# A reordered chunk plan, banks for the token range, later rotations, and the compressed layers' weights behind the gates' first slot

## The chip, the cores and the metric

The kernel runs on one core of a Trainium2 chip. The metric is the device time of one execution in microseconds (us), the median of three runs. The five engines of the core are told of by their names in the profile: PE is TensorE's matmul (PEld its weight load), DVE is VectorE, ACT is ScalarE, POOL is GpSimd, and SP is SyncE, which here only issues transfers.

## The reference

Two transformer blocks on a batch of one, 256 tokens of width 1024, all in float32. The first mixes a three-group attention and an RWKV-like recurrence, with a feed-forward layer and a gated embedding behind them. The second, on which most of the change lies, begins so:

```python
p = _split_columns(u @ w_in)          # q_a k_a v_a q_b k_b ... q_c k_cmp v_cmp k_sel v_sel ... g_merge
o_a = _stick_breaking(q_a, k_a, v_a)
o_b = _dsa_attention(_rope(q_b), rope1(k_b), v_b, _rope(q_idx), rope1(k_idx), w_idx)
o_c = _nsa_attention(_rope(q_c), rope1(k_cmp), v_cmp, rope1(k_sel), v_sel, rope1(k_win), v_win, gates_c, cmp...)
g = sigmoid(g_merge)                  # 3 x 1024 columns
merged = g[0] * (o_a @ w_up[0]) + g[1] * (o_b @ w_up[1]) + g[2] * (o_c @ w_up[2])
```

and inside `_nsa_attention` keys and values are compressed: 15 overlapping blocks of 32 tokens by 64 features go through `gelu(blocks @ w1) @ w2`, with w1 of 2048 by 128 (1 MB) once for keys and once for values.

## The kernel before, in words

**Products in parts.** A float32 product is made of three matmuls on rounded parts: each operand is split into a high part (written by ScalarE, line 1808, type fp32r) and a low part (VectorE subtracts the high part from the whole, line 2705), and TensorE takes high x high, high x low and low x high (lines 716 to 718, or 794, 795 and 803). So before TensorE can use a weight slot, three things happen in a row: its transfer lands, ScalarE copies it, VectorE subtracts. Both do so in halves of the contraction, `(j, 0)` and `(j, 1)`. The high parts have two buffers, so the split of slot j waits for the last matmul of slot j - 2.

**Streams and slots.** The weights of a stage are a stream of slots of up to 1 MB, held in a ring of three places; SP loads them in order (`load`, line 610), each one waiting until TensorE has finished the slot that held the place before. For the second block's input projection (`st2`) the slots are: 0 to 4, the feature chunks n = 2 to 6 of `plan_2` (features on the partitions, 256 tokens in the free dimension); 5 and 6, the token range (tokens on the partitions, 464 columns: values, gates' inputs, index weights); 7 to 18, six gate column ranges of two slots each. Chunks n = 0 and 1 were made in `head`, before.

**Feature chunks.** A chunk of 256 columns has two halves of 128, one of 128 columns has one. Behind a chunk, ScalarE reads the bank (one plain copy and four that swap 32-row groups, `rope_read`), and VectorE rotates it one chunk later with cosines, sines and an add (`rope`, lines 2806, 2808 and 2810). Chunk n = 4 is the third group's query, n = 5 the four single keys (k_b, k_idx, k_sel, k_win in 64-column pieces), n = 6 the compressed layers' input (128 columns). Chunks and token range take banks 0 and 1 in turn.

**The early split.** `ahead` (scalar program): for slot 5 of `st2`, ScalarE makes the first half's high part before it reads the chunk of n = 5, not after.

**Key copies.** `scores` needs the single keys in both halves of the partitions. ScalarE copies three times behind the chunk n = 6, VectorE three times when it reads the token range (`read_vt`).

**Turns.** The gates are then computed by `turns.drive(gates_main(), nsa_keys(), dsa(1), dsa(0), stick())`. Every engine runs the same schedule: one step of the main work (on TensorE six matmuls of a gate slot, four steps to a slot), then one step of a side work, the four sides in turn. So turn 1 is a step of slot 7 and a step of `nsa_keys`, turn 2 a step and `dsa(1)`, turn 3 with `dsa(0)`, turn 4 with `stick`, and turn 5 begins slot 8 with `nsa_keys` again. All engines execute in order. In turns 1 and 2, ScalarE's main step is the split of slot 8 in two halves; after the second, in turn 2, it applies the ReLU to the scores of `dsa(1)`. The sides share the banks 2, 3 and 4 in rotation: `dsa(1)` takes 2 and 3, `dsa(0)` 4 and 2.

**The compressed layers.** `nsa_keys`: POOL adds the position vector for 15 blocks (line 3837) once the rotation of the compressed input is there. In its second step (turn 5), TensorE takes 64 small products of the blocks with w1 (line 1597) into banks 5 and 6, in four row groups of 32; in its fourth step (turn 13) it turns and sums these groups with eight products against pieces of the identity (line 1607), then two last products. The transfers of w1 (four of 512 KB, in rows of 512 bytes) and of w2 (four of 32 KB) are issued on SP behind slot 1 (`if j == 1`, line 669), in practice at the start of the stage. The gate ranges from the third on write where w1 lay and wait for its products.

**The first block's part.** While TensorE works on the q/k chunks of the first block (`qkv`, six chunks), the RWKV recurrence runs beside them as side work in an order written out by hand (`order_1`); its masked copies on VectorE are lines 2993 and 2969. VectorE rotates chunk n - 1 at the end of chunk n (`rope1`), in two buffers `rt1`.

**Activation tables.** ScalarE loads a table set before a function that the current set does not hold; the stick-breaking side uses Abs, Exp and Ln in turn 12.

Of the kernel before, what the change touches and what calls it, by code (L numbers as in the profile page):

```python
# [33 lines left out]
C_END = C_SINC + 256  # L34
# [10 lines left out]
def shape_constants():  # L45
# [37 lines left out]
    c[0:64, C_SINC:C_SINC + 256] = np.concatenate([-sin, sin])  # L83
    return c
# [189 lines left out]
def program(nc, A, consts, vecs, pt, out):  # L274
    with ExitStack() as ctx:
# [75 lines left out]
        sm_nsa = [(small(4), small(4), small(4), small(4)) for _ in range(2)]  # L351
        sm_mem = [(small(4), small(4), small(4)) for _ in range(2)]
# [36 lines left out]
        rt1 = [view3(P + 9216 + 1024 * i, 2, 256) for i in range(2)]  # L389
# [36 lines left out]
        def rope_to(n):  # L426


            return RC[:, 6:10:3, :] if n == 5 else RC[:, 10:11, :] if n == 6 else RC[:, 2 * (n - 2):2 * (n - 2) + 2, :]
# [45 lines left out]
        def rslot3(n, nk, width):  # L475
# [8 lines left out]
                  ([(1152, 256, 0)], [128, 128]), ([(1476, 256, 0)], [128, 128]),  # L484
                  ([(1024, 64, 0), (1408, 64, 64), (1860, 64, 128), (1988, 64, 192)], [128, 128]), ([(1732, 128, 0)], [128])]
# [111 lines left out]
        def sync_program(e):  # L597
# [105 lines left out]
        def tensor_program(e, turns):  # L703
# [131 lines left out]
            def token_range(st, j0, n, w, freed, late):  # L835
                nk = 8 // n
                banks = [next(pg), next(pg)]
# [700 lines left out]
            def scores(done, name, i, qc, kc_, W, freed):  # L1538
# [3 lines left out]
                q.wait_ge(*rope_dve.at("in2", 5))  # L1542
# [44 lines left out]
            def nsa_keys():  # L1587
                yield
# [30 lines left out]
            def nsa(i):  # L1619
# [7 lines left out]
                q.wait_ge(*rope_dve.at("in2", 4))  # L1627
# [167 lines left out]
        def scalar_program(e, turns):  # L1795
# [78 lines left out]
            def ahead(st, j):  # L1874

                return st.tag == "st2" and j == 5
# [13 lines left out]
            def token_range(st, j0, n, read):  # L1890
                nk = 8 // n
                banks = [next(pg), next(pg)]
                for s in range(n):
                    for i in range(2):
                        for r in range(nk // 2):
                            if i == 0 and (r == 1 or r == 0 and not ahead(st, j0 + s + 1)):
# [85 lines left out]
            def rope_read(tag, n, m, b, zs, dst):  # L1982
                if n >= (2 if tag == "qk" else 4):
                    q.wait_ge(*rope_dve.at(tag, n - 2))
# [4 lines left out]
            def qkv():  # L1989
# [9 lines left out]
                for n in range(6):  # L1999
                    b = next(pg)  # L2000
                    yield from feature_chunk(st1, QK_AT + n, [128, 128], lambda: rope_read("qk", n, 2, b, rt1[n % 2], qk[:, 2 * n:2 * n + 2, :]))
# [358 lines left out]
            def read2(n, b):  # L2360
                if n < 2:
                    copy(QA[:, 2 * n:2 * n + 2, :], halves(bank(b))).then_inc(main_act.up("qa", n), 1)
                else:
                    m = 1 if n == 6 else 2
# [4 lines left out]
            def read_vt(i, p):  # L2369
                copy(vt[:, i, 0:256], p[:, 0:256])  # L2370
                act(g12[:, 12 * i:12 * i + 12], p[:, 448:460], ACT.Tanh, scale=0.5).then_inc(main_act.up("vt2", i), 1)

            def main_b():
                for n in range(2, 7):
                    b = next(pg)
                    yield from feature_chunk(st2, n - 2, plan_2[n][1], lambda: read2(n, b))
                    if n == 6:
                        q.wait_ge(*rope_dve.at("in2", 5))
                        for m, half in enumerate(half_rows[::-1]):
                            copy(RC[half, 7, :], RC[half_rows[1], 6, :]).then_inc(key_act.up(m), 1)  # L2380
                        q.wait_ge(*key_act.at(1))
                        copy(RC[half_rows[1], 6, :], RC[half_rows[0], 6, :]).then_inc(key_act.up(2), 1)
                yield from token_range(st2, 5, 2, read_vt)

            turns.alone(main_b())


# [228 lines left out]
        def vector_program(e, turns):  # L2616
# [127 lines left out]
            def token_range(st, j0, n, read, late):  # L2744
                nk = 8 // n
                banks = [next(pg), next(pg)]
# [64 lines left out]

            def rope1(n):
                rope("qk", n, 2, rt1[n % 2], qk[:, 2 * n:2 * n + 2, :], C_COS, C_SIN)

            def qkv():
# [474 lines left out]
            def rope2(n):  # L3290
                if n >= 2:
                    m = 1 if n == 6 else 2
                    rope("in2", n, m, rz2[n % 2][:, 0:m, :], rope_to(n), *((C_COSC, C_SINC) if n == 6 else (C_COS, C_SIN)))

            def read_vt(i, p):
                if i == 0:
                    q.wait_ge(*rope_dve.at("in2", 5))
# [9 lines left out]
            def main_b():  # L3307
# [3 lines left out]
                yield from token_range(st2, 5, 2, read_vt, lambda: rope2(6))  # L3311
# [341 lines left out]
        def gpsimd_program(e, turns):  # L3653
# [177 lines left out]
            def nsa_keys():  # L3831
# [3 lines left out]
                q.wait_ge(*rope_dve.at("in2", 6))  # L3835
# [126 lines left out]
```

## Time and profile before

| | |
|---|---|
| median of 3 runs | 909.4 us (909.09 to 910.02) |
| the profiled execution | 909.91 us |
| its span | 907.4 us |
| TensorE busy | 882.2 us, 97% |
| VectorE busy | 606.8 us, 67% |
| ScalarE busy | 480.5 us, 53% |
| transfers | 150.71 MB, mean 166 GB/s |

The span is what the profile shows of the execution; the time has 2.5 us more around it. In the timeline, a row is: start, duration, engine, line, operation, output and input, shape, count, and in brackets how long the engine had been idle and what ended it. Rows of one kind next to each other are merged, and the duration is then that of all. A window's row is: from and to, its length, the busy time (and instructions) of PE, PEld, DVE, ACT and POOL, PE's granted clock as a share of 2.4 GHz, the DMA share and the GB/s.

### The profile page before, as it was taken

What the parts mean: (1) busy time and instruction counts of PE and PEld (TensorE: products, weight loads), DVE (VectorE), ACT (ScalarE), POOL (GpSimd) and SP (SyncE); (2) the same over time, 40 slices, a digit from 0 to 9 for tenths busy, and PEclk for the clock granted to TensorE, in tenths of its full rate; (3) what the DMA queues carried; (4) which work ended last, traced back from release to release, by engine and by line L of the source; (5) the groups of instructions that cost most, each with busy time, mean ns of one, the idle gap of its engine ahead of it and who ended that gap; (6) DMA issues with size and microseconds to landing.
All of it is one profiled execution on the core that took longest, in us unless ns stands there. A gap on an engine that the chain in (4) does not pass through costs nothing.

```text
span 907.4 us, 15435 instructions
## 1 busy us (share of the span) xinstructions
PE 882.2 (97%) x6552; PEld 748.8 (83%) x6552; DVE 606.8 (67%) x976; ACT 480.5 (53%) x775; POOL 29.2 (3%) x51
## 2 busy tenths in 40 slices
PE   7999999999899999999999999999999999999997
PEld 4999898787689888888889978776788788888885
DVE  4578978557856666656766577877863566666673
ACT  4775667436534444456444856484622545555561
POOL 0010000010000000000000020000000000000000
PEclk9999999999999999999999999999999999999999
DMA  9644333224468665555339764353817566665521
GB/s 336 190 140 140 99 119 114 63 83 150 178 248 282 188 190 190 200 202 187 121 112 229 164 210 144 111 186 107 277 38 206 146 187 188 191 193 194 199 95 47
DMA packets 131204, 150.71 MB, mean 166 GB/s; under 512 B 11808, under 2 KB 102176, under 8 KB 131008
## 3 DMA queue, kind: packets, MB, share of 16 engines
q1 hardware_dynamic: 129920, 145.57, 51.8%
q10 hardware_dynamic: 1216, 4.16, 1.2%
q8 instruction: 52, 0.85, 0.4%
q14 instruction: 16, 0.13, 0.0%
HBM read 148.67 MB, written 1.05 MB: 165 GB/s over the span
## 4 chain that ended last, share of the span: by engine, by line
PE 85%; DVE 7%; ACT 4%; issue 2%; DMA 1%; POOL 0%; POOLq 0%; ACTq 0%; DVEq 0%
PE psum L821 12%; PE psum L716 9%; PE psum L718 9%; PE psum L717 9%; PE psum L826 7%; PE psum L774 4%; PE psum L794 3%; PE psum L795 3%; PE psum L803 3%; PE psum L722 3%; PE psum L870 2%; PE psum L880 2%; PE psum L871 2%; PE psum L827 2%; DVE parts L2705 2%
## 5 line engine op out<-in xcount | busy, mean ns | idle before, releaser
L1808 ACT ACTIVATE parts<-low 128x1024 fp32r<-128x1024 f32 (+3 forms) x252 | 254.3, 1044 | 65.6 <-PE psum L718 48.3
L2705 DVE TENSOR_TENSOR parts<-low,parts 128x1024 fp32r<-128x1024 f32 (+3 forms) x156 | 183.7, 1206 | 37.7 <-ACT parts L1808 37.5
L716 PE MATMUL psum<-parts 128*128 128x512 f32 (+2 forms) x424 | 169.1, 399 | 4.6 <-DVE parts L2705 2.5
L718 PE MATMUL psum<-parts 128*128 128x512 f32 (+2 forms) x424 | 163.5, 386 | 0.0
L717 PE MATMUL psum<-parts 128*128 128x512 f32 (+2 forms) x424 | 163.4, 385 | 0.0
L1808 ACT ACTIVATE high<-psum 128x512 f32<-128x512 f32 (+6 forms) x115 | 63.4, 560 | 134.2 <-PE psum L827 76.4
L821 PE MATMUL psum<-parts 128*128 128x512 f32 x462 | 116.8, 392 | 0.0
L716 PEld LDWEIGHTS psum<-parts 128*128 128x128 f32 x424 | 79.6, 188 | 26.3 <-DVE parts L2705 4.5
L821 PEld LDWEIGHTS psum<-parts 128*128 128x128 f32 x462 | 86.9, 188 | 16.9
L718 PEld LDWEIGHTS psum<-parts 128*128 128x128 f32 x424 | 79.6, 188 | 16.4
L717 PEld LDWEIGHTS psum<-parts 128*128 128x128 f32 x424 | 79.8, 188 | 13.9
L2770 DVE TENSOR_TENSOR parts<-low,parts 128x1024 fp32r<-128x1024 f32 x54 | 66.0, 1222 | 35.3 <-ACT parts L1808 35.3
L794 PE MATMUL psum<-parts 128*128 128x256 f32 (+2 forms) x312 | 79.0, 291 | 0.0
L795 PE MATMUL psum<-parts 128*128 128x256 f32 (+2 forms) x312 | 76.5, 282 | 0.0
L826 PEld LDWEIGHTS psum<-parts 128*128 128x128 f32 x528 | 72.0, 190 | 5.1
L826 PE MATMUL psum<-parts 128*128 128x256 f32 x528 | 73.6, 282 | 0.0
L794 PEld LDWEIGHTS psum<-parts 128*128 128x128 f32 (+2 forms) x312 | 58.9, 189 | 2.2 <-issue 1.2
L795 PEld LDWEIGHTS psum<-parts 128*128 128x128 f32 (+2 forms) x312 | 59.0, 189 | 0.3 <-issue 0.3
L3197 DVE TENSOR_TENSOR mid<-psum,high 128x512 f32<-128x512 f32 x33 | 22.8, 692 | 46.2 <-ACT high L1808 46.2
L1808 ACT ACTIVATE mid<-psum 32x512 f32<-32x512 f32 (+7 forms) x61 | 32.9, 552 | 31.5 <-PE psum L803 12.9
L803 PE MATMUL psum<-parts 128*128 128x256 f32 (+2 forms) x312 | 43.8, 283 | 0.0
L803 PEld LDWEIGHTS psum<-parts 128*128 128x128 f32 (+2 forms) x312 | 40.1, 189 | 0.0
(313 smaller groups left out, 1310.6 us busy)
## 6 DMA issues: line engine op xcount, KB each, us to landing
low<-in_w_in_dram SPq DMA_DIRECT2D x40, 1024.0 KB, 5.3
low<-in_w_ffn_in_dram SPq DMA_DIRECT2D x44, 512.0 KB, 5.2
low<-in_w_ff_in_dram SPq DMA_DIRECT2D x16, 1024.0 KB, 5.7
low<-in_w_ff_out_dram SPq DMA_DIRECT2D x16, 1024.0 KB, 4.8
low<-in_w_ffn_out_dram SPq DMA_DIRECT2D x11, 1024.0 KB, 5.0
low<-in_w_out_dram SPq DMA_DIRECT2D x8, 1024.0 KB, 5.2
low<-in_w_ple_gate_dram SPq DMA_DIRECT2D x4, 1024.0 KB, 5.0
low<-consts_dram ACTq DMA_DIRECT2D x1, 2078.0 KB, 9.0
```

What stands on the lines that cost most here:

```text
L716: mm(o, l[0], r[0], start, False)
L717: mm(o, l[0], r[1], False, False)
L718: return mm(o, l[1], r[0], False, stop)
L774: t = mm(PSUM[0:m, banks[n], 256 * j + 128 * i:256 * j + 128 * i + 128], w3[:, k, off:off + m], uT[:, k, 128 * i:128 * i + 128], k == 0, k ...
L794: mm(o, hi[:, k, c], st.uh[:, k, :], k == 0, False)
L795: mm(o, lo_[:, k, c], st.uh[:, k, :], False, False)
L803: t = mm(o, hi[:, k, c], st.ul[:, k, :], False, k == 7)
L821: mm(p, hi[:, k, c], st.u2(k), k == 0, False)
L826: mm(p[:, 0:256], lo_[:, k, c], st.uh[:, k, :], False, False)
L1808: return e.activation(o, a, ACT.Copy)
L2705: tt(rslot3(n, nk, width)[:, r, 0:w], slot3(n, nk, width)[:, r, 0:w], st.hi3(j)[:, r, 0:w].bitcast(F32), ALU.subtract) \
L2770: tt(rview(OR + 2048 * n + 1024 * (k % 2), 1024), slot(n)[:, 1024 * (k % 2):1024 * (k % 2) + 1024], rview(base, 1024).bitcast(F32), ALU.su ...
```

## The change

- In `plan_2` the order of the last three chunks becomes: single keys (n = 4, slot 2), compressed input (n = 5, slot 3, 128 columns), third group's query (n = 6, slot 4). What depends on the numbers (`rope_to`, the waits of `scores` and `nsa`, POOL's wait, `read_vt`) follows.
- The token range of `st2` uses banks 5 and 6.
- `ahead` is gone: every split comes in the plain order.
- ScalarE's three key copies move from behind the last chunk into `read_vt`, row block 0.
- The first step of `nsa_keys` on TensorE no longer yields, so its 64 products come in turn 1 instead of turn 5; a yield is added behind them, so the later steps keep their turns.
- The summing of the four row groups takes one product per half against a selection matrix `C_SEL` (128 more columns of constants, 64 KB) instead of four.
- The transfers of w1 and w2 are issued behind slot 7 instead of slot 1.
- In the first block, `rt1` has four buffers, and `turned_at` sets which rotations stand at the end of chunk n: none, none, 0, 1, 2 and 3, 4 (and 5 in the gates, as before).
- One Exp of one column (`first_exp`) on ScalarE ahead of the turns.

```diff
-C_END = C_SINC + 256
+C_SEL = C_SINC + 256
+C_END = C_SEL + 128
...
+    c[:, C_SEL:C_SEL + 16] = r % 32 == s[:, 0:16]
...
-        rt1 = [view3(P + 9216 + 1024 * i, 2, 256) for i in range(2)]
+        rt1 = [view3(P + 8704 + 512 * i, 2, 256) for i in range(4)]
...
         plan_2 = [([(0, 256, 0)], [128, 128]), ([(256, 256, 0)], [128, 128]), ([(768, 256, 0)], [128, 128]),
-                  ([(1152, 256, 0)], [128, 128]), ([(1476, 256, 0)], [128, 128]),
-                  ([(1024, 64, 0), (1408, 64, 64), (1860, 64, 128), (1988, 64, 192)], [128, 128]), ([(1732, 128, 0)], [128])]
+                  ([(1152, 256, 0)], [128, 128]), ([(1024, 64, 0), (1408, 64, 64), (1860, 64, 128), (1988, 64, 192)], [128, 128]),
+                  ([(1732, 128, 0)], [128]), ([(1476, 256, 0)], [128, 128])]
...
                 load(("st2", j), (3, 0, 5)[j % 3], [cols(*p) for p in pieces], main_pe.at("st2", j, 1))
-                if j == 1:
+                if j == 7:
                     q.wait_ge(*wo_pe.at("pg", "y", 1, 1))
...
-                yield from token_range(st2, 5, 2, 464, lambda i: [main_act.at("vt2", i), main_dve.at("vt2", i)], nothing)
+                yield from token_range(st2, 5, 2, 464, lambda i: [main_act.at("vt2", i), main_dve.at("vt2", i)], nothing, (5, 6))
...
             def nsa_keys():
-                yield
                 p = [bank(5), bank(6)]
...
                 yield
                 yield
+                yield
                 p = bank(7)
                 for h in range(2):
                     q.wait_ge(*cmp_dve.at("x", h))
-                    for g in range(4):
-                        t = mm(p[:, 16 * h:16 * h + 16], hd[:, h, :], ident[:, 32 * g:32 * g + 16], g == 0, g == 3)
+                    t = mm(p[:, 16 * h:16 * h + 16], hd[:, h, :], const(C_SEL, 16), True, True)
...
                 for n in range(steps):
-                    if n == 1 or n == 0 and not ahead(st, j + 1):
+                    if n < 2:
                         split(st, j + 1, (n,))
                     yield
                 q.wait_ge(*main_pe.at(st.tag, j, 1))
-                if ahead(st, j + 2):
-                    split(st, j + 2, (0,))
                 read()
...
             def read_vt(i, p):
+                if i == 0:
+                    q.wait_ge(*rope_dve.at("in2", 4))
+                    for m, half in enumerate(half_rows[::-1]):
+                        copy(RC[half, 7, :], RC[half_rows[1], 6, :]).then_inc(key_act.up(m), 1)
+                    q.wait_ge(*key_act.at(1))
+                    copy(RC[half_rows[1], 6, :], RC[half_rows[0], 6, :]).then_inc(key_act.up(2), 1)
...
             turns.alone(main_b())
+            act(first_exp, ident[:, 0:1], ACT.Exp).then_inc(stick_act.up("table"), 1)
...
+            turned_at = ((), (), (0,), (1,), (2, 3), (4,))
...
-                    yield from feature_chunk(st1, QK_AT + n, [128, 128], (lambda n=n: rope1(n - 1)) if n else nothing, nothing)
+                    yield from feature_chunk(st1, QK_AT + n, [128, 128], lambda n=n: [rope1(m) for m in turned_at[n]], nothing)
```

## Rows read from the trace of the kernel before

**Rows 1.** The page, busy time of the engines, share of the span, instructions

```profile
PE 882.2 (97%) x6552; PEld 748.8 (83%) x6552; DVE 606.8 (67%) x976; ACT 480.5 (53%) x775; POOL 29.2 (3%) x51
```

**Rows 2.** Timeline of TensorE and VectorE in the first block's q/k chunks

```profile
103.72 1.12 PE L803 MATMUL psum<-parts 128*128 128x256 f32 x8
105.87 0.24 PE L1203 MATMUL psum<-high 64*64 64x64 f32 x1 [1.04 <-DVE high L2993]
107.19 0.24 PE L1203 MATMUL psum<-mid,high 64*64 64x64 f32 x1 [0.16 <-DVE high L2969]
...
100.95 0.69 DVE L2806 TENSOR_TENSOR mid<-mid,low 128x512 f32<-128x512 f32 x1
102.88 2.84 DVE L2993 TENSOR_TENSOR high<-psum,low 64x512 f32<-64x512 f32 x4
...
133.82 2.85 DVE L2993 TENSOR_TENSOR high<-psum,low 64x512 f32<-64x512 f32 x4 [2.62 <-PE psum L1181]
```

**Rows 3.** Timeline of the second block's chunks and token range

```profile
502.20 2.01 ACT L1808 ACTIVATE parts<-low 128x1024 fp32r<-128x1024 f32 x2
503.29 2.36 DVE L2705 TENSOR_TENSOR parts<-low,parts 128x1024 fp32r<-128x1024 f32 x2 [5.96 <-ACT parts L1808]
510.81 3.02 ACT L1808 ACTIVATE high<-psum 128x512 f32<-128x512 f32 x5 [0.84 <-PE psum L803]
515.42 1.12 PE L803 MATMUL psum<-parts 128*128 128x256 f32 x8
518.30 1.12 PE L803 MATMUL psum<-parts 128*128 128x256 f32 x8
520.66 0.48 PE L716 MATMUL psum<-parts 128*128 128x464 f32 x1 [1.24 <-ACT high L1808]
522.82 0.48 PE L716 MATMUL psum<-parts 128*128 128x464 f32 x1 [0.63 <-DVE parts L2705]
528.37 0.48 PE L716 MATMUL psum<-parts 128*128 128x464 f32 x1 [1.49 <-DVE parts L2705]
```

**Rows 4.** SP's issue, two issues with us to landing, two windows

```profile
486.56 2.47 SPq L669 DMA_DIRECT2D high<-in_cmp_w_v_dram  x1
high<-in_cmp_w_v_dram SPq DMA_DIRECT2D x1, 512.0 KB, 11.5
low<-in_w_in_dram SPq DMA_DIRECT2D x1, 1024.0 KB, 4.9
488.00:494.00 6.00, 6.00 (x55) 6.00 (x55) 4.10 (x4) 3.13 (x6) 0.00 (x0) 1.00 1.21 203
529.00:531.00 2.00, 2.00 (x11) 1.78 (x10) 1.97 (x4) 0.80 (x1) 2.00 (x4) 1.00 1.04 406
```

**Rows 5.** Timeline of the turns and the blocks; two lines' ns min/median/max, starts

```profile
536.37 1.13 PE L1548 MATMUL psum<-high 64*128 64x256 f32 x8
539.01 0.38 PE L1548 MATMUL psum<-high 64*128 64x128 f32 x2
537.53 1.09 ACT L1804 ACTIVATE mid<-psum 128x512 f32<-128x512 f32 x2 [1.44 <-PE psum L1548]
525.90 6.09 POOL L3837 TENSOR_TENSOR mid<-high,low 128x32 f32<-128x32 f32 x15 [41.46 <-DVE high L2810]
L1597 PE MATMUL psum<-high,mid x128: 269/269/293, 544.7 to 546.4; 64*32 64x128 f32 x128
L1607 PE MATMUL psum<-low,mid x16: 177/263/263, 557.6 to 559.2; 128*128 128x16 f32 x16
```

**Rows 6.** Timeline of table load and last matmul; two windows (clock third last)

```profile
554.94 1.28 ACT L1804 ACT_TABLE_LOAD   x1
901.01 0.39 PE L718 MATMUL psum<-parts 128*128 128x512 f32 x1
...
560.56:583.60 23.04, 22.21 (x118) 17.28 (x117) 21.12 (x63) 10.97 (x18) 0.00 (x0) 1.00 0.32 100
904.00:905.00 1.00, 0.00 (x0) 0.00 (x0) 0.30 (x1) 0.46 (x1) 0.00 (x0) 0.56 0.00 0
```

More of the change, by code:

```diff
@@ L351, in program @@
         sm_nsa = [(small(4), small(4), small(4), small(4)) for _ in range(2)]
+        first_exp = small(1)
         sm_mem = [(small(4), small(4), small(4)) for _ in range(2)]
@@ L426, in rope_to @@
         def rope_to(n):
-            return RC[:, 6:10:3, :] if n == 5 else RC[:, 10:11, :] if n == 6 else RC[:, 2 * (n - 2):2 * (n - 2) + 2, :]
+            return RC[:, 6:10:3, :] if n == 4 else RC[:, 10:11, :] if n == 5 else RC[:, 4:6, :] if n == 6 else RC[:, 2 * (n - 2):2 * (n - 2) + 2, :]
         vt = view3(P + 21760, 2, 660)
@@ L833, in wide_chunk, with token_range @@
                 yield
-            def token_range(st, j0, n, w, freed, late):
+            def token_range(st, j0, n, w, freed, late, banks=None):
                 nk = 8 // n
-                banks = [next(pg), next(pg)]
+                banks = banks or [next(pg), next(pg)]
                 for s in range(n):
@@ L1541, in scores @@
                     bank(b)
-                q.wait_ge(*rope_dve.at("in2", 5))
+                q.wait_ge(*rope_dve.at("in2", 6))
                 q.wait_ge(*key_act.at(2))
@@ L1626, in nsa @@
                     bank(b)
-                q.wait_ge(*rope_dve.at("in2", 4))
+                q.wait_ge(*rope_dve.at("in2", 6))
                 q.wait_ge(*cmp_act.at("kc"))
@@ L1872, in head @@
                             read(n)
-            def ahead(st, j):
-                return st.tag == "st2" and j == 5
             def feature_chunk(st, j, widths, read):
@@ L1884, in feature_chunk, with token_range @@
                 q.wait_ge(*main_pe.at(st.tag, j, 1))
-                if ahead(st, j + 2):
-                    split(st, j + 2, (0,))
                 read()
                 yield
-            def token_range(st, j0, n, read):
+            def token_range(st, j0, n, read, banks=None):
                 nk = 8 // n
-                banks = [next(pg), next(pg)]
+                banks = banks or [next(pg), next(pg)]
                 for s in range(n):
@@ L1895, in token_range @@
                         for r in range(nk // 2):
-                            if i == 0 and (r == 1 or r == 0 and not ahead(st, j0 + s + 1)):
+                            if i == 0 and r < 2:
                                 split(st, j0 + s + 1, (r,))
@@ L1982, in rope_read @@
             def rope_read(tag, n, m, b, zs, dst):
-                if n >= (2 if tag == "qk" else 4):
-                    q.wait_ge(*rope_dve.at(tag, n - 2))
+                if n >= 4:
+                    q.wait_ge(*rope_dve.at(tag, n - (4 if tag == "qk" else 2)))
                 z = halves(bank(b))[:, 0:m, :]
@@ L2000, in qkv @@
                     b = next(pg)
-                    yield from feature_chunk(st1, QK_AT + n, [128, 128], lambda: rope_read("qk", n, 2, b, rt1[n % 2], qk[:, 2 * n:2 * n + 2, :]))
+                    yield from feature_chunk(st1, QK_AT + n, [128, 128], lambda: rope_read("qk", n, 2, b, rt1[n % 4], qk[:, 2 * n:2 * n + 2, :]))
             def gate(r):
@@ L2363, in read2 @@
                 else:
-                    m = 1 if n == 6 else 2
+                    m = 1 if n == 5 else 2
                     rope_read("in2", n, m, b, rz2[n % 2][:, 0:m, :], rope_to(n))
@@ L2376, in main_b @@
                     yield from feature_chunk(st2, n - 2, plan_2[n][1], lambda: read2(n, b))
[L2377 to L2383, printed above, removed]
+                yield from token_range(st2, 5, 2, read_vt, (5, 6))
             turns.alone(main_b())
+            act(first_exp, ident[:, 0:1], ACT.Exp).then_inc(stick_act.up("table"), 1)
             pa2 = itertools.cycle((2, 3, 4))
@@ L2742, in feature_chunk, with token_range @@
                 yield
-            def token_range(st, j0, n, read, late):
+            def token_range(st, j0, n, read, late, banks=None):
                 nk = 8 // n
-                banks = [next(pg), next(pg)]
+                banks = banks or [next(pg), next(pg)]
                 for s in range(n):
@@ L3291, in rope2 @@
                 if n >= 2:
-                    m = 1 if n == 6 else 2
-                    rope("in2", n, m, rz2[n % 2][:, 0:m, :], rope_to(n), *((C_COSC, C_SINC) if n == 6 else (C_COS, C_SIN)))
+                    m = 1 if n == 5 else 2
+                    rope("in2", n, m, rz2[n % 2][:, 0:m, :], rope_to(n), *((C_COSC, C_SINC) if n == 5 else (C_COS, C_SIN)))
             def read_vt(i, p):
                 if i == 0:
-                    q.wait_ge(*rope_dve.at("in2", 5))
+                    q.wait_ge(*rope_dve.at("in2", 4))
                     for m, half in enumerate(half_rows):
@@ L3310, in main_b @@
                     yield from feature_chunk(st2, n - 2, plan_2[n][1], lambda: rope2(n - 1), nothing)
-                yield from token_range(st2, 5, 2, read_vt, lambda: rope2(6))
+                yield from token_range(st2, 5, 2, read_vt, lambda: rope2(6), (5, 6))
             turns.alone(main_b())
@@ L3834, in nsa_keys @@
                 e.memset(blk[:, :, 15:32], 0.0).then_inc(cmp_pool.up("pad"), 1)
-                q.wait_ge(*rope_dve.at("in2", 6))
+                q.wait_ge(*rope_dve.at("in2", 5))
                 for n in range(15):
```

2 lines of the change are left out of this document (1 added, 1 removed).

## The prediction

> **What bounds the kernel now.** Read first the page's busy times, then the rows in which TensorE had nothing to do. TensorE is busy 97% of the span [rows 1], so a microsecond of its work or of its idleness is nearly a microsecond of the kernel; the other engines matter only where TensorE waits for them. The change touches two stretches where it does. A wait in the rows counts from the modelled end of the matmul before, which overlaps the next one by about 0.2 us; I therefore price waits from start to start.
>
> In the first block's q/k chunks, TensorE stops at 105.87 and 107.19 for VectorE [rows 2]. Eight products at L803 take 1.05 us to the next start (0.13 each), so without the waits the products at 105.87 would begin at 104.8. VectorE was late because it ran the rotation of q/k chunk 0 (100.95 to 102.9, three operations of 0.69) before the masked copies at 102.88.
>
> In the second block's chunks, a half chunk (128 columns of weight) takes TensorE 2.88 us, from 515.42 to 518.30 [rows 3], a whole one 5.76. The last ends at 519.3. The token range after it begins at 520.66, 1.4 late (its bank is still being read by ScalarE); it stops again at 522.82, 0.8, and at 528.37, 1.65, for VectorE's low parts [rows 3]. Together 3.8 us.
>
> **The change, step by step.** Times are those of the profile of before, so that the shifts can be added.
>
> *Rotations in the first block.* Rotation 0 goes one chunk later, and the masked copies start when the low parts are done, at about 100.95 instead of 102.88: 1.9 us earlier. Both TensorE waits (1.1 + 0.2) go: **-1.3**. Chunk 4 gets two rotations, 2.0 us more on VectorE; the cover is the 2.62 us in which VectorE idles before 133.82 [rows 2]. Without it, up to 2 us would return.
>
> *Banks 5 and 6 for the token range, the key copies moved into it, the early split given up.* The bank wait goes, and since the query chunk is now last, the other two waits change form. The old 3.8 us are taken out, **-3.8**, and the new ones counted:
>
> The half chunk is now the last but one. ScalarE reads chunk n=4 from 510.81 for 3.02 us and only then splits the weights of n=6, 1.0 us per half, VectorE taking 1.2 for each low part [rows 3]: first low part at 510.81 + 3.02 + 1.0 + 1.2 = 516.1. TensorE finishes the half chunk at 513.4: **+2.7**, and +0.1 for the second part. The query chunk ends at 516.1 + 0.1 + 5.8 = 522.0. ScalarE reads it until 525.1; VectorE finishes its rotation (two more operations of 0.65) and then the low part of slot 6 (1.1) at 527.6. TensorE has done slot 5 (24 matmuls at 0.21) at 527.1: **+0.6**. Slot 6 ends at 532.9, and the first turn's six matmuls at 534.4.
>
> *The compressed layers' weights.* They leave SP's queue ahead of the chunks' weights (no TensorE wait there hangs on a load) and enter it behind slot 7. Slot 7's load waits for the query chunk's last matmul, so it goes out at 522.1. Between issue and landing of a lone 1 MB load lie 4.9 us, 2.6 of them data at 406 GB/s, so 2.3 us are not [rows 4]. The four 512 KB transfers run in rows of 512 bytes at 203 GB/s [rows 4]: 2.1 MB take 10.4 us. The four small ones I put at 0.8, between 0.3 at 406 and 1.3 at half of 203 (their rows are 256 bytes). Then the up-projection's 1 MB and slot 8's 1 MB, 2.6 each. One queue serves them in order, so the compressed weights land near 522.1 + 2.3 + 2.6 + 10.4 = 537.4, and slot 8 at 537.4 + 0.8 + 5.2 = 543.4. What SP is held up by its full queue is inside this: the last quarter's issue began at 486.56, and it landed 11.5 us after [rows 4], so SP runs ahead of the data.
>
> *Who waits.* TensorE reaches the compressed products at 534.4 and stands about 3.1 us. POOL's blocks, 6.1 us [rows 5] from about 522.7, are done; the reads of banks 5 and 6 end about a microsecond after slot 6. But behind slot 8 hangs more: ScalarE, in order, splits slot 8 in turns 1 and 2 before the ReLU that frees the bank which `dsa(0)` wants in turn 3. Landing 543.4, two splits 2.0, one ReLU 0.55 (half of 1.09 [rows 5]): the bank is free at 546.1. Unhindered, TensorE would be there earlier: the `dsa(1)` scores and six matmuls take 2.64 (536.37 to 539.01), 1.1 of it the scores, the compressed products 2.0 (544.7 to 546.4 and the last one's 0.27) [rows 5]; 534.4 + 2.0 + 1.6 + 2.6 = 540.7, with 0.1 for the changes of kind. So the two stops together are **+5.4**, whatever part of them the first takes. Slot 8's low parts are ready before its matmuls at 550.1, and the loads of 9 and 10 follow in time (546 for a need near 550).
>
> *Small products.* Moving them to turn 1 costs nothing by itself. The hidden rows' turning falls from eight products (16 passes, 557.6 to 559.3 [rows 5]) to two: 1.7 x 6/8 = **-1.3**. From 560.56, where ScalarE's Ln lets it go, VectorE is busy 21.1 of 23.0 us [rows 6]; this saving is kept only if that chain also moves. The early Exp does that: it shifts one table load (1.28 us at 554.94 [rows 6]) to before turn 1, where ScalarE waits for slot 8 anyway. Bounds: kept 1.3, or nothing. I take it kept. The constants' 64 KB more are 0.2 us of queue under other loads, the rest has one answer: nothing.
>
> Sum: -1.3 - 3.8 + 2.8 + 0.6 + 5.4 - 1.3 = **+2.4 us**. The profiled execution took 909.9 us, 907.4 of it span, half a microsecond above the median of 909.4; on the median the forecast is 911.8.
>
> **Rivals.** *The transfers run faster than 203 GB/s.* The 203 were measured for these very rows, and the queue was full; against it speaks only that wider rows reach 406 [rows 4]. At that pace they take 5.2, not 10.4, slot 8 lands at 538.2, the bank is free at 540.9, and 0.2 us are left of the 5.4: 909.4 - 2.8 = 906.6, faster. It decides once slot 8 has landed by 538, where its ReLU no longer ends behind TensorE's arrival at 540.7. The Trainium skill, in "DMA: Bandwidth & Descriptors", section Bandwidth, measured 341 GB/s for a 1 MB transfer; by that figure, an estimate, the four would take 6.2 us and the kernel 907.7. No run here shows that pace for rows of 512 bytes.
>
> *TensorE's clock falls in the stop.* At the end of the kernel the last matmul starts at 901.01; at 904 to 905 the granted clock is 0.56, on its way from 2.4 to 1.2 GHz [rows 6]. A stop of 3.1 us is about as long. At half clock the 6.3 us of work up to the second stop would take 12.6, of which the second stop (2.3) swallows that much: at most +4.0, 915.8. If the low clock lasts through 2.3 us of work or less, it costs nothing. "TensorE: Matmul & The Clock Gate", section on the HAM clock gate, in the Trainium skill says that an idle stretch halves the clock until TensorE has been busy again for a while; the trace's fall to 0.56 agrees, and no row here shows a fall between two stages.
>
> *VectorE's full stretch eats the small gains.* If the table load stays where it is, or the compressed products' earlier place leaves VectorE behind, the 1.3 are lost and up to 1 us more: 913.1 to 914.1. For it speaks that VectorE is so full there [rows 6]; against it that ScalarE's 1.28 match TensorE's 1.3.
>
> *The stops are smaller than counted*, because the queue takes the transfers partly side by side, half of the 5.4: 909.1, no change.
>
> **How the numbers follow.** A measurement can tell 0.2%, 1.8 us: faster is below 907.6, slower above 911.2. My forecast has 0.60 (its own range 910.8 to 913.4, from landing times of slot 8 off by 1 us and the early Exp at half its worth; 0.05 of it falls within 0.2%), the fast transfers 0.11 (0.09 faster, 0.02 same), the clock 0.09, VectorE 0.11, the smaller stops 0.09. That makes faster 0.09, same 0.16, slower 0.75. For the range I leave out most of the fast case and the clock's upper end: 908.9 to 914.8.
>
> **What would show it.** Right: no wait at the old 105.87; a TensorE wait of 2.5 us for VectorE before the query chunk; none for ScalarE at the token range's start; a wait of about 3 us ahead of L1597's products, released by the DMA of the compressed weights; a second of about 2.3 us at a score product, released by ScalarE's ReLU, with ScalarE idle about 9 us for slot 8's load; no table load between Abs and Exp. Wrong: slot 8's landing less than 17 us after the query chunk, or a clock below 1.00 after the first stop.

## The result, and the profile after

The changed kernel takes **915.4 us** (median of 4 runs, 913.8 to 915.99) against 909.5 of the kernel before on the same chip: a ratio of 1.0064, 95% interval 1.0052 to 1.0076. It is slower, as forecast, but by 5.9 us where the forecast had 2.4, and the time lies 0.6 above the range. The profiled execution took 915.99 us, its span 914.0, so it stands 6.6 above the span of before; the ledger below explains those 6.6.

The page of the changed kernel, which answers to [rows 1]:

```profile
PE 884.0 (97%) x6540; PEld 749.9 (82%) x6540; DVE 606.7 (66%) x976; ACT 480.6 (53%) x776; POOL 26.6 (3%) x51
```

TensorE is busy 1.8 us longer with twelve matmuls fewer. Some matmuls must have become slower; the other 4.8 us are idle time. The timeline of TensorE, the answer to [rows 3]:

```profile
516.27 0.36 PE L797 MATMUL psum<-parts 128*128 128x256 f32 x1 [2.67 <-ACT high L1810]
516.46 0.28 PE L798 MATMUL psum<-parts 128*128 128x256 f32 x1
...
517.71 0.41 PE L797 MATMUL psum<-parts 128*128 128x256 f32 x1
517.92 0.41 PE L798 MATMUL psum<-parts 128*128 128x256 f32 x1
...
519.41 1.47 PE L806 MATMUL psum<-parts 128*128 128x256 f32 x8
...
523.59 0.37 PE L719 MATMUL psum<-parts 128*128 128x464 f32 x1
...
529.35 0.48 PE L719 MATMUL psum<-parts 128*128 128x464 f32 x1 [0.55 <-DVE parts L2702]
```

The token range's start no longer waits, and the query chunk waits instead. Its first matmuls follow each other at 0.12 us, those from 516.85 to 519.4 at 0.21. The windows show why (clock third from the end):

```profile
513.00:516.00 3.00, 0.60 (x6) 0.40 (x4) 1.10 (x1) 2.94 (x5) 0.00 (x0) 1.00 1.16 284
516.00:517.00 1.00, 0.73 (x5) 0.76 (x6) 1.00 (x2) 0.96 (x3) 0.00 (x0) 0.88 1.04 348
517.00:518.00 1.00, 1.00 (x7) 1.00 (x6) 1.00 (x3) 0.95 (x4) 0.00 (x0) 0.50 1.20 293
...
519.00:520.00 1.00, 1.00 (x6) 1.00 (x6) 1.00 (x2) 0.65 (x1) 0.00 (x0) 0.50 0.07 9
520.00:521.00 1.00, 1.00 (x10) 1.00 (x9) 1.00 (x2) 0.00 (x0) 0.00 (x0) 0.91 0.00 0
```

From about 516.8 to 520.2, starting half a microsecond after TensorE has resumed from its stop, the granted clock is 0.50, 1.2 instead of 2.4 GHz. The chunk takes 7.32 us (516.27 to 523.59) instead of the 5.76 of before.

The turns, TensorE, ScalarE and SP's issue, the answer to [rows 4, 5]:

```profile
539.68 2.90 PE L1599 MATMUL psum<-high,mid 64*32 64x128 f32 x128 [3.64 <-DMA high<-in_cmp_w_v_dram]
542.51 0.80 PE L719 MATMUL psum<-parts 128*128 128x512 f32 x1
...
549.00 0.71 PE L1551 MATMUL psum<-high 64*128 64x128 f32 x8 [1.46 <-ACT mid L1806]
...
535.18 1.28 ACT L1806 ACT_TABLE_LOAD   x1
536.47 0.20 ACT L1806 ACTIVATE low<-low 128x1 f32<-128x1 f32 x1
546.46 2.00 ACT L1810 ACTIVATE parts<-low 128x1024 fp32r<-128x1024 f32 x2 [9.79 <-DMA low<-in_w_in_dram]
548.37 1.06 ACT L1806 ACTIVATE mid<-psum 128x512 f32<-128x512 f32 x2
...
523.79 0.37 SPq L613 DMA_DIRECT2D low<-in_w_in_dram  x1
524.20 1.44 SPq L672 DMA_DIRECT2D high<-in_cmp_w_k_dram  x2
525.68 6.07 SPq L672 DMA_DIRECT2D high<-in_cmp_w_v_dram  x2
```

Both stops are where they were forecast and for the reasons forecast. Slot 8 reaches ScalarE at 546.46, not 543.4. The clock is at 0.50 once more, from 540.7 to 544.1: the small products take 2.83 us from start to start (539.68 to 542.51) instead of 1.96 in the kernel before. That fall costs nothing, because the second stop ends when ScalarE is ready, however fast TensorE gets there.

### The profile page after: what moved, and what is told of

Its sections match the earlier page's. It is cut to its first block, busy times and chain, and to the rows that moved or that the text cites. A ratio compares the mean times of both kernels' runs of the same rounds, so it can differ in the third digit from the quotient of the medians.

```text
span 914.0 us, 15410 instructions
## 1 busy us (share of the span) xinstructions
PE 884.0 (97%) x6540; PEld 749.9 (82%) x6540; DVE 606.7 (66%) x976; ACT 480.6 (53%) x776; POOL 26.6 (3%) x51
## 3 DMA queue, kind: packets, MB, share of 16 engines
HBM read 148.73 MB, written 1.05 MB: 164 GB/s over the span
## 4 chain that ended last, share of the span: by engine, by line
PE 84%; DVE 7%; ACT 3%; DMA 2%; issue 2%; SPq 1%; POOL 0%; POOLq 0%; ACTq 0%; DVEq 0%
PE psum L824 12%; PE psum L719 9%; PE psum L721 8%; PE psum L720 8%; PE psum L829 7%; PE psum L797 4%; PE psum L777 4%; PE psum L798 3%; PE psum L806 3%; PE psum L725 3%; PE psum L873 2%; PE psum L883 2%; PE psum L874 2%; DVE parts L2702 2%; PE psum L830 2%
## 5 line engine op out<-in xcount | busy, mean ns | idle before, releaser
L1810 ACT ACTIVATE parts<-low 128x1024 fp32r<-128x1024 f32 (+2 forms) x252 | 254.2, 1044 | 74.9 <-PE psum L721 48.2
L2702 DVE TENSOR_TENSOR parts<-low,parts 128x1024 fp32r<-128x1024 f32 (+2 forms) x156 | 183.5, 1206 | 44.6 <-ACT parts L1810 44.3
L797 PE MATMUL psum<-parts 128*128 128x256 f32 (+2 forms) x312 | 80.1, 293 | 2.7 <-ACT high L1810 2.7
L798 PE MATMUL psum<-parts 128*128 128x256 f32 (+2 forms) x312 | 77.6, 285 | 0.0
L797 PEld LDWEIGHTS psum<-parts 128*128 128x128 f32 (+2 forms) x312 | 59.6, 191 | 5.0 <-ACT high L1810 2.8
L798 PEld LDWEIGHTS psum<-parts 128*128 128x128 f32 (+2 forms) x312 | 59.8, 192 | 0.3 <-issue 0.3
L806 PE MATMUL psum<-parts 128*128 128x256 f32 (+2 forms) x312 | 44.1, 284 | 0.0
L806 PEld LDWEIGHTS psum<-parts 128*128 128x128 f32 (+2 forms) x312 | 40.5, 191 | 0.0
```

The costliest lines, as they stand in the source:

```text
L797: mm(o, hi[:, k, c], st.uh[:, k, :], k == 0, False)
L798: mm(o, lo_[:, k, c], st.uh[:, k, :], False, False)
L806: t = mm(o, hi[:, k, c], st.ul[:, k, :], False, k == 7)
L1810: return e.activation(o, a, ACT.Copy)
L2702: tt(rslot3(n, nk, width)[:, r, 0:w], slot3(n, nk, width)[:, r, 0:w], st.hi3(j)[:, r, 0:w].bitcast(F32), ALU.subtract) \
```

## The experiments

Experiments 1 to 3 ask what the late transfers cost and how, 4 asks for the first block's part, 5 to 7 for the stop before the query chunk, 8 and 9 for the small products, and 10 and 11 for slot 8's landing. "Before" is always the kernel before, on the same chip. A distance from the changed kernel's 915.4 or between two experiments can be one between chips; on all of them the kernel before took 909.2 to 909.5.

**1. Transfers back behind slot 1, all else as changed.**

```diff
-                if j == 7:
+                if j == 1:
```

> The changed kernel with one line put back: the compressed layers' transfers are issued behind slot 1 again. Theory T (the transfers behind slot 7 cost both stops in the turns): the wait of 3.64 us for the compressed weights and the one of 1.46 us for ScalarE's ReLU go, 6.9 us from start to start, so 915.4 - 6.9 = 908.5 us; the stop of 2.7 us before the query chunk stays, and with it the fall of TensorE's clock, which now nothing downstream hides. Rival C (the new chunk order and the clock make the loss, the transfers are hidden anyway): 913 us or more.

Measured: 910.2 us, ratio to before 1.0010 (1.0002 to 1.0019). The late transfers cost 5.2 us net, and both stops in the turns are gone. What the expectation (908.5) missed is a stop elsewhere, shown by TensorE's timeline, and behind it the old one; ScalarE's row shows what the first waited for:

```profile
506.19 0.36 PE L797 MATMUL psum<-parts 128*128 128x256 f32 x1 [1.62 <-DVE parts L2702]
...
517.83 0.36 PE L797 MATMUL psum<-parts 128*128 128x256 f32 x1 [2.65 <-ACT high L1810]
...
536.77 2.02 PE L1599 MATMUL psum<-high,mid 64*32 64x128 f32 x128 [0.48 <-DVE low L2623]
...
503.73 2.00 ACT L1810 ACTIVATE parts<-low 128x1024 fp32r<-128x1024 f32 x2 [1.87 <-DMA low<-in_w_in_dram]
```

Slot 2 was as large before and stood behind the same 2.1 MB, and nobody waited for it. But then it was one piece of 256 columns, and the transfers ran at 303 and 349 GB/s from 497 to 499; now it is the keys' four pieces of 64 columns, in rows of 256 bytes, and the same two microseconds show 181 and 134. That the row size sets this pace is argued, no run varies it alone. Experiment 6 takes up the place in the queue.

**2. The kernel before, transfers behind slot 7.** The same line, `j == 1` made `j == 7`; the small products stay in turn 5.

> The kernel before with only the transfers moved behind slot 7; the compressed products stay in turn 5. Theory T (the price is set by slot 8's landing, through ScalarE's ReLU in turn 3, not by the wait for the compressed weights): no TensorE wait for the weights in turn 5, but one of 6 to 7.5 us in turn 3; 909.5 + 6 to 7.5 = 915.5 to 917 us. Rival W (the loss is the wait of the first turn for the weights themselves): with the products in turn 5 the weights are there, and the time stays within 1 us of 909.5.

Measured: 919.8 us, 10.5 above before, ratio 1.0112 (1.0099 to 1.0126). No product waits for its weights; the price is the wait behind slot 8 and ScalarE, as theory T has it, and 3 us that the expectation (915.5 to 917) lacked:

```profile
546.26 1.23 PE L1548 MATMUL psum<-high 64*128 64x128 f32 x8 [6.74 <-ACT mid L1804]
547.42 0.79 PE L716 MATMUL psum<-parts 128*128 128x512 f32 x1
```

Its windows around and behind that stop:

```profile
543.00:546.00 3.00, 0.00 (x0) 0.00 (x0) 1.19 (x1) 2.28 (x3) 0.00 (x0) 0.50 0.86 315
546.00:552.00 6.00, 5.74 (x23) 4.48 (x25) 4.42 (x10) 2.91 (x6) 0.00 (x0) 0.50 0.11 18
553.00:556.00 3.00, 3.00 (x94) 2.34 (x99) 2.98 (x5) 0.00 (x0) 0.00 (x0) 1.00 0.57 221
```

Of the 10.2 us of span, 6.7 are the stop and 3 are lost in some 6 us of work at half clock behind it (546.3 to 552.6). The other 0.5 was lost far from the edit, where the clock also fell, behind a stop that the kernel before has too (1.75 us there, without a fall):

```profile
230.73 0.51 PE L1395 MATMUL psum<-parts 128*128 128x512 f32 x1 [1.84 <-ACT mid L1804]
...
232.00:233.00 1.00, 1.00 (x3) 0.73 (x3) 0.96 (x3) 0.74 (x2) 0.00 (x0) 0.50 1.04 403
```

**3. The changed kernel, small products back in turn 5.** A `yield` ahead of them, one fewer behind.

> The changed kernel with the compressed products back in turn 5, transfers still behind slot 7. Theory T: the stop in turn 1 goes, TensorE stops in turn 3 instead until the same moment, and the products, which lay in front of that stop, now cost their 2.0 us behind it: 917 us, or some 0.5 less where the clock stays up. Rival W (the loss is the wait in turn 1): 3.6 us faster, 911.8 us.

Measured: 920.0 us, ratio 1.0117 (1.0101 to 1.0132), 4.6 slower than with the products in turn 1 and 3 above what was expected. One stop of 8.06 us takes the place of two (3.64 and 1.46) with work between them, and the work behind it runs at half clock up to 550.8. TensorE's timeline, then a window:

```profile
547.26 1.23 PE L1551 MATMUL psum<-high 64*128 64x128 f32 x8 [8.06 <-ACT mid L1806]
...
558.11 0.41 PE L1600 MATMUL psum<-high,mid 64*32 64x128 f32 x4 [1.63 <-issue]
```

```profile
547.00:550.00 3.00, 2.74 (x12) 2.23 (x13) 2.15 (x6) 1.35 (x4) 0.00 (x0) 0.50 0.00 0
```

In turn 5 the products also meet a wait of 1.63 that the profile gives no releaser for. So moving them is worth something here: 2.0 us by filling a stop with work, and 1.6 if the wait, seen in one trace, belongs to turn 5. The low clock behind the one stop costs another 1.7, where the changed kernel's fell between its two stops and cost nothing. In a kernel without that stop they fill nothing.

**4. The kernel before, with the later rotations only** (`rt1` with four buffers, `turned_at`).

> The kernel before with only the later rotations of the first block and their four buffers. The forecast's own step says -1.3 us: 908.2 us, the waits at 105.87 and 107.19 gone. Theory I (the lead is lost again within the first block, in places where TensorE waits for its own issue): the two waits go, but by 260 us the lead is 0 to 0.2, and the time is 909.3 to 909.5 us.

Measured: 908.8 us, ratio 0.9994 (0.9985 to 1.0002), 0.5 less at the median and not clear of no change: neither the forecast's -1.3 nor theory I's 0 to 0.2. Compared by the start of the same matmul, TensorE leads the kernel before by 1.3 us at 107, 0.45 at 124, 1.05 at 129, 0.7 at 139 and 0.65 at the end of the profiled execution. Two gaps on the way:

```profile
117.50 0.21 PE L1203 MATMUL psum<-mid,high 64*64 64x64 f32 x1 [0.28 <-issue]
...
138.67 0.21 PE L1204 MATMUL psum<-high 64*64 64x64 f32 x1 [0.57 <-issue]
```

Both are in runs of 64-column products that wait for nothing the profile shows. The first is not there in the kernel before, and the lead drops by 0.5 at it. The second was 0.25 before, but it is no effect of the edit: experiments 8, 9 and 11, whose first block is untouched, have 0.55, 0.54 and 0.51 at that place, and experiment 6 has 0.25. Experiment 8's row:

```profile
139.31 0.21 PE L1207 MATMUL psum<-high 64*64 64x64 f32 x1 [0.55 <-issue]
```

In the profile of the changed kernel the lead is 1.4 at 107, 0.3 at 139 and 0.0 at 259. That is one execution: over the eight profiles with the later rotations the lead at 500 is 0.0, 0.0, 0.3, 0.35, 0.6, 0.6, 1.0 and 1.05, mean 0.5, and over four without them (experiments 2, 8, 9, 11) -0.5, 0.3, -0.35 and 0.25.

**5. The changed kernel without the stop before the query chunk.** Slot 4 is split before the keys' chunk is read (ScalarE side shown), and the query chunk gets bank 4.

```diff
-                    if n < 2:
+                    if n < 2 and (st.tag, j) != ("st2", 3):
...
                 q.wait_ge(*main_pe.at(st.tag, j, 1))
+                if st.tag == "st2" and j == 2:
+                    split(st, j + 2)
                 read()
```

> The changed kernel with both halves of slot 4 (the query chunk's weights) split before ScalarE reads the chunk of the single keys, and the query chunk in bank 4, whose reader is long done; the compressed layers' transfers stay behind slot 7. It asks what the stop of 2.83 us before the query chunk costs in all. Theory C (a stop of this length brings TensorE's clock down, as the trace of the changed kernel shows with 3.41 us at 0.50 right behind it): the stop and the 1.5 us by which the chunk was longer both go, less about 0.6 us of new small waits for VectorE: 915.4 - 4.3 + 0.6 = 911.7 us, and the granted clock at 516 to 520 stays 1.00. Rival N (the clock fell for another reason, for instance at that point of the time or with the load of the chip, and not because of the stop): only the stop goes, 915.4 - 2.8 + 0.6 = 913.2 us, and the clock is again at 0.50 for 3.4 us somewhere in the chunks. Rival S (the wait only moves: VectorE or the transfer behind it is late next, in the query chunk or at slot 5): over 914 us.

Measured: 912.7 us (912.0 to 913.7), ratio 1.0040 (1.0026 to 1.0053): 2.7 below the changed kernel. That is also the bare length of the stop and lies nearer to rival N (913.2) than to theory C (911.7). The timeline and windows speak for C:

```profile
519.99 0.48 PE L719 MATMUL psum<-parts 128*128 128x464 f32 x1 [0.64 <-DVE parts L2706]
...
544.30 0.71 PE L1552 MATMUL psum<-high 64*128 64x128 f32 x8 [1.83 <-ACT mid L1807]
544.95 0.71 PE L719 MATMUL psum<-parts 128*128 128x512 f32 x1
```

```profile
545.00:548.00 3.00, 3.00 (x8) 1.96 (x8) 2.89 (x6) 0.77 (x3) 0.00 (x0) 0.51 0.03 8
```

No chunk ran at the low clock; the token range starts at 519.99, 3.6 us before 523.59, which is the 2.83 and the 1.5, less the new 0.64. The bank in turn 3 is free 4.7 us earlier (544.30 for 549.00). Of the 4.7 only 3.2 are left in the span (910.8 for 914.0). The rest is a clock fall behind the second stop, of which there was none in the changed kernel's profile, and behind which no further stop swallows it. One trace without a fall in the chunk does not prove that the fall hangs on the stop; experiment 6 bears on that.

**6. Transfers behind slot 2 (`j == 2`), stop left in.**

> The changed kernel with the compressed layers' transfers issued behind slot 2 instead of slot 7. The run with them behind slot 1 gave 910.2 us and had a stop of 1.62 us before the four-piece keys, whose slot 2 lands behind them, and 2.65 before the query chunk. Theory Q (slot 2 was late because it stood behind 2.1 MB in the one queue): with the transfers behind slot 2, that stop goes, slot 3 (half the size, needed one chunk later) is not late, and the time is 910.2 - 1.7 = 908.5 us. Rival: the lateness passes on to slot 3 or 4, whose chunk then stops for as long: 910 us or more.

Measured: 909.1 us, ratio 0.9996 (0.9987 to 1.0005), 1.1 below experiment 1. The stop at slot 2 is gone and no other slot is late: theory Q (908.5 expected). Its 11 executions fall in two sets. Two had a mean granted clock of 0.999 and took 907.35 and 907.95 us; nine had 0.997 or 0.998 and took 908.7 to 909.9. The profiled one is of the two, and has the stop but no fall:

```profile
515.33 0.36 PE L797 MATMUL psum<-parts 128*128 128x256 f32 x1 [2.67 <-ACT high L1810]
```

```profile
515.00:519.00 4.00, 3.67 (x30) 3.65 (x31) 3.96 (x6) 3.63 (x7) 0.00 (x0) 1.00 0.85 210
```

The same stop of 2.67 us is followed by a fall in one execution and not in another. Six profiles have a stop of 2.65 to 2.67 us: a fall follows in four (the changed kernel, experiments 3, 5 and 10) and none in two (experiments 1 and 6). The medians of the two sets lie 1.5 us apart, the size of the 1.5 in the changed kernel's profile. That the slower nine are the ones with a fall is likely but not shown: six of the 21 executions of the kernel before on this chip also had a mean clock of 0.997, and took 909.0 to 909.6 like the others.

**7. Both edits.**

> Both edits of the two runs above together: transfers behind slot 2, and slot 4's halves split before the keys' chunk is read, with the query chunk in bank 4. If the two costs are separate and add up, 908.5 - 2.8 + 0.6, and less about 1.0 for clock falls in the executions that had them: 905.3 to 906.3 us, faster than both kernels. If one of the two takes the other's place (the wait goes to VectorE or to a late slot), 908 us or more.

Measured: **905.4 us** (904.97 to 905.58), ratio 0.9956 (0.9943 to 0.9968): faster than both kernels, 3.9 us under before (909.2) and 10.1 under the change. The two costs were separate, and with the stop gone the five executions agree within 0.6 us, all at 0.998 or 0.999 (the 21 of before on this chip within 0.9). ScalarE's order, and what is left of TensorE's waits in this stretch:

```profile
510.19 2.01 ACT L1811 ACTIVATE parts<-low 128x1024 fp32r<-128x1024 f32 x2 [1.70 <-PE psum L806]
512.22 4.99 ACT L1811 ACTIVATE high<-psum 128x512 f32<-128x512 f32 x10
...
519.42 0.48 PE L719 MATMUL psum<-parts 128*128 128x464 f32 x1 [0.63 <-DVE parts L2706]
...
531.89 2.02 PE L1600 MATMUL psum<-high,mid 64*32 64x128 f32 x128 [0.48 <-DVE low L2627]
```

Split first, then two chunks read in a row; 1.1 us of waits where before had 3.4 [rows 3].

**8. The kernel before with the selection matrix and the early Exp.**

```diff
-                    for g in range(4):
-                        t = mm(p[:, 16 * h:16 * h + 16], hd[:, h, :], ident[:, 32 * g:32 * g + 16], g == 0, g == 3)
+                    t = mm(p[:, 16 * h:16 * h + 16], hd[:, h, :], const(C_SEL, 16), True, True)
...
+            act(first_exp, ident[:, 0:1], ACT.Exp).then_inc(stick_act.up("table"), 1)
```

> The kernel before with the selection matrix (two products instead of eight when the hidden rows are turned) and the early Exp, and nothing else. The prediction's term is -1.3 us: 908.1 us, the table load no longer between Abs and Exp, and 4 matmul passes instead of 16. Rival V (VectorE's full stretch behind it takes the gain, or TensorE waits there as long as before): 909.3 us, no change. Rival X (the early Exp costs ScalarE 1.28 us at a place where it is late): 910 us or more, with a new TensorE wait for ScalarE in turns 1 to 3.

Measured: 907.8 us, ratio 0.9984 (0.9976 to 0.9993). The term stands: -1.4 for -1.3.

**9. The same without the early Exp.**

> The kernel before with the selection matrix alone, without the early Exp. With both the time was 907.8 us, 1.4 below before. The prediction took the gain of 1.3 us as kept only because the early Exp moves ScalarE's table load of 1.28 us out of the stick-breaking chain. Theory E (that is so): without it VectorE's and ScalarE's chain ends as late as before, TensorE waits for it, and the time is 909.2 us, no change. Rival (the chain follows TensorE and the table load was hidden anyway): 907.9 us, as with both.

Measured: 909.1 us, ratio 0.9997 (0.9988 to 1.0005). Theory E: eight products become two (16 passes become 4), and the gain is lost to a wait for ScalarE and a longer one for VectorE. The line's own row (durations in ns, as in [rows 5]), and from the timeline ScalarE's table load, which stands between the stick-breaking side's functions as before [rows 6], and TensorE's waits:

```profile
L1608 PE MATMUL psum<-low,mid x4: 177/262/263, 558.0 to 558.2; 128*128 128x16 f32 x4
```

```profile
555.26 1.28 ACT L1805 ACT_TABLE_LOAD   x1
...
565.17 0.48 PE L718 MATMUL psum<-parts 128*128 128x512 f32 x1 [0.40 <-ACT high L1805]
...
568.06 0.50 PE L718 MATMUL psum<-parts 128*128 128x512 f32 x1 [0.81 <-DVE parts L2706]
```

With the Exp (experiment 8) the second was 0.47 and the first was not there; in the kernel before the second was 0.41. By the start of the same matmul, experiment 9 is 0.3 us behind the kernel before at 512 and 0.3 at its end, so it gains nothing in this stretch; experiment 8 goes from 0.3 ahead to 1.75 ahead.

**10. The changed kernel, slot 9 held back until slot 8 has landed.**

```diff
+                if j == 9:
+                    q.wait_ge(*slot_in[SLOT["st2", 8]].at("st2", 8))
```

> The changed kernel with one wait more on SP: slot 9's load is issued only once slot 8 has landed. In the changed kernel slot 9 went out 0.5 us behind slot 8 and slot 8 landed 3.9 us after the transfer ahead of it, where the prediction had 2.6. Theory B (the two share the queue's engines, so the one in front is slowed by the one behind): slot 8 lands 1.3 us earlier, at about 2.6 us after the transfer ahead of it, the stop in turn 3 shrinks from 1.46 to about 0.2, and the time is 915.4 - 1.4 = 914.0 us; slot 9 lands near 550, still before it is split. Rival F (slot 8's own pace behind the 512-byte rows is 3.9 us, whoever follows): no change, 915.4 us.

Measured: 915.3 us (913.2 to 918.0), ratio 1.0067 (1.0049 to 1.0084). Theory B falls: the stop in turn 3 is 1.45, as it was. But the run shows slot 8 alone at the end of the queue, and so where the time is. GB/s in this profile for each microsecond from 520, then SP's issue of slot 7 and ScalarE's first split of slot 8:

```profile
GB/s 0 0 0 0 41 264 408 388 248 202 200 198 197 229 202 192 199 198 240 360 414 385 387 387 43 10 0 127 330 406 186 16 141 379 406 119 12 0 0 59
```

```profile
523.46 0.37 SPq L613 DMA_DIRECT2D low<-in_w_in_dram  x1
...
546.14 2.00 ACT L1812 ACTIVATE parts<-low 128x1024 fp32r<-128x1024 f32 x2 [9.77 <-DMA low<-in_w_in_dram]
```

From 524 to 545 the row adds up to 5.38 MB, which is all that was issued up to slot 8. The data flow from about 524.9 to 544.1, 19.2 us; ScalarE can start 2.0 us later.

**11. The kernel before, transfers behind slot 8 (`j == 8`).**

> The kernel before with the compressed layers' transfers issued behind slot 8 instead of slot 1. Behind slot 7 the same kernel took 919.8 us (10.3 above before), with one stop of 6.7 us in turn 3 that waited for ScalarE's ReLU behind slot 8's split. Theory T (what costs is that slot 8 stands behind these transfers, not that they come late themselves): slot 8 lands before ScalarE wants it, the turn-3 stop goes, the compressed weights land near 543 to 545, just ahead of turn 5's products at 544.7 or up to 1 us behind, and slot 9 is in time: 909.2 to 910.5 us. Rival L (the late transfers cost wherever they stand, because slot 9 or the products are late next): 913 us or more.

Measured: 910.25 us, ratio 1.0010 (1.0001 to 1.0018). One slot's place in the queue is the difference between +10.5 (experiment 2) and +0.8. TensorE's timeline has no stop in turn 3 and no wait for the weights in turn 5; what is left among the small products is this:

```profile
546.76 0.41 PE L1597 MATMUL psum<-high,mid 64*32 64x128 f32 x4 [0.49 <-issue]
```

## Why the prediction was wrong, step by step

The sign and the two stops with their releasers were right, and the sum was short by 4.2 us of span (+2.4 forecast, +6.6 measured). Three steps carry it (1.5 + 1.3 + 1.3), and the first is a term that the sum put at nothing.

**The clock in the query chunk, +1.5.** The prediction had a rival in which TensorE's clock falls, gave it 0.09, and looked only at the stop in turn 1, where the second stop swallows the loss. The stop before the query chunk, which it had sized itself at 2.7 us (2.83 from start to start), was not weighed at all. Its own row could have said that this length can do it: the last matmul of the kernel before ends at 901.40, and 0.56 in the window from 904 to 905 [rows 6] puts the fall some 2.7 us after that. Behind the stop stands no other but a chain: the chunk's end releases slot 7's load, and everything up to turn 3 hangs on that. Experiment 5 took the stop away and no low clock came in the chunk; by the six profiles under experiment 6 the same stop is followed by a fall in some executions and not in others, so that it came in the changed kernel's profile is in part chance. "TensorE: Matmul & The Clock Gate" in the Trainium skill, section "HAM oscillation — how this bites in real kernels", names a length of idle gap to stay under, and 2.7 us stay under it; the falls behind stops of 2.66 and 2.67 us disagree, and they decide.

**Slot 8's landing, +1.3.** Forecast 543.4, measured 546.46. Of the 3.1, 1.7 are a later start (the clock again, slot 7's issue at 523.79 and not 522.1). The data took 19.2 us in experiment 10 where the terms add up to 19.0 (2.6 + 10.4 + 0.8 + 5.2), so the 203 GB/s and the serial queue were right and the fast-transfer rival falls. What failed is "2.3 us are not" data: it came from a lone load; here it was 1.4 us from issue to first data and 2.0 from last data to ScalarE. The Trainium skill, in "DMA: Bandwidth & Descriptors", section "Anatomy of one DMA — SWDGE (gpsimd) path", puts most of a transfer's fixed cost at its end, for another way of issuing than SP's; the 2.0 of 3.4 us agree. From 546.46 on, the step is exact: two splits of 2.0 and one ReLU of 0.55 give 549.0, and TensorE resumes at 549.00.

**The rotations, +1.3.** Both waits went as said, and the cover of 2.62 us held, since no wait for VectorE came in its place. But -1.3 was booked as kept to the end. The changed kernel's profile has nothing of it left at 259; experiment 4 kept 0.5, and 0.5 is the mean lead of the eight profiles with this edit. So some 0.8 of the 1.3 is the step's error, and the rest is the luck of this execution. The step counted the waits that were visible and took the rest of the stretch as fixed. The gap at 117.50 (experiment 4) takes 0.5 back; the cause of it and of the rest stays open.

**What held.** The token range: its 3.8 went, and of the new waits the one at slot 6 was 0.55 for 0.6 and the one ahead of the query chunk 2.83 for 2.8. The two stops were worth 5.4 by the sum; in the profile they are 5.1 of idleness (3.64 and 1.46) and, with the clock, 1.6 of slower work between them, and moving the transfers to behind slot 2 gave 6.4 (915.4 to 909.1). The small products with the early Exp gave 1.4 for 1.3, and experiment 9 shows the reason given was right: without the Exp 0.3 is left (909.1 for 909.45), inside the interval.

**What the sum hid.** Of the change, only the place of the transfers and the order that puts ScalarE's read ahead of the split cost time. With these two put right the rest is a gain of 3.9 us: 0.5 rotations, 1.4 small products and Exp, and by difference about 2.0 for chunk order, banks and turn.

## What to carry to other kernels

In one queue, ask for each bulk transfer what stands behind it and which in-order engine will sit on that: in the kernel before, 2.1 MB moved to behind slot 7 cost 10.5 us, to behind slot 8 only 0.8. Where an engine both empties a finished bank and prepares the next weights, let it prepare first and send the next chunk to another bank. Price a stop of TensorE of about 2.7 us by its length plus 1.5 us for a clock fall that may or may not come (here four times in six), and one of 6.7 us by its length plus 3, unless another stop behind it waits for something that TensorE's pace does not move.

## What was not expected of the hardware

- The clock fell to 0.50 behind a stop of 2.67 us in one execution and not in another (515.33 in experiment 6), and behind shorter ones too: 1.83 us, some 6 us after an earlier fall had ended (experiment 5), and 1.84 us with no other stop of its length near it (230.73 in experiment 2), where twelve other profiles have 1.5 to 1.8 us and no fall.
- In stops of up to 3.64 us the fall came not in the stop but 0.2 to 1.4 us after TensorE had resumed (0.5 in the changed kernel's query chunk, 1.4 in experiment 3's). In those of 6.74 and 8.06 us it came inside, 2.9 and 4.7 us after the last matmul.
- On the chip of experiments 5 to 8, the two kernels with a stop of 2.7 us spread over 1.7 and 2.6 us between executions (experiments 5 and 6), those without over 0.6 to 1.0 (before, experiments 7 and 8). On other chips the kernel before alone spread over 1.9 and 2.6, so the spread is no sign of a stop by itself.
- The length of a stop does not set how much work runs slowly behind it: some 6 us behind a stop of 6.74 (experiment 2), 3.5 behind one of 8.06 (experiment 3), 3.4 behind 3.64.
- Between the last data of a 1 MB transfer and the engine that waited for it lay 2.0 us, with nothing else in the queue (experiment 10).
- A lead that TensorE won in the stretch of small products shrank again without a wait on any other engine that grew as much (1.3 to 0.65 us in experiment 4), and profiles of one first block differ by up to 1.05 us in what is left of it.
